# Experts of a two-layer decoder trunk: indirect DMAs for tokens and results, half of the weight loads issued by ACT, last block reordered

## The reference, cut to what matters

```python
top_logit, top_idx = lax.top_k(logits, TOP_K)          # TOP_K = 2
top_w = jax.nn.softmax(top_logit, axis=-1)
gate = jnp.einsum('tk,tke->te', top_w, jax.nn.one_hot(top_idx, N_EXPERTS, dtype=jnp.float32)).astype(u.dtype)
for e in range(N_EXPERTS):                             # 8 experts
    out = out + gate[:, e:e + 1] * swiglu(t, w_gate[e], w_up[e], w_down[e])
# swiglu: (silu(u @ w_gate) * (u @ w_up)) @ w_down, 1024 -> 3584 -> 1024
```

## Time and profile before

| | us |
|---|---|
| median of 3 runs | 1657.75 |
| lowest and highest | 1656.53, 1658.16 |
| the profiled execution's own time | 1658.17 |
| its span in the trace | 1656.4 |
| start of the item loop on PE, to the end of the last load's matmuls | 620.4 to about 1608.4 |

### The profile page before, as it was taken

The page is one execution under the profiler, slowest core; times in us unless marked ns, Lnnn a source line. Parts: engine busy times, 40 slices in busy tenths (PEclk is TensorE's granted clock), DMA queues, the critical chain, the costliest instruction groups (busy, mean ns, idle before and its releaser), DMA issues.

```text
span 1656.4 us, 21473 instructions
## 1 busy us (share of the span) xinstructions
PE 1571.4 (95%) x8127; PEld 1331.4 (80%) x8127; DVE 1293.3 (78%) x1102; ACT 1028.5 (62%) x865; POOL 17.9 (1%) x36
## 2 busy tenths in 40 slices
PE   5997999999799779999999999999999999999996
PEld 4986788887788668888888888888888888888885
DVE  4976744448686577888888888888888889889885
ACT  3545543346354636777677677677677677677663
POOL 4000000000000000000000000000000000000000
PEclk9998999999899879999999999999999999999998
DMA  7431365555344038999999999999999999999970
GB/s 232 152 128 51 110 207 200 178 178 179 126 128 140 7 115 304 376 339 358 375 339 358 375 340 358 374 341 356 375 343 356 374 342 357 374 341 358 371 277 25
DMA packets 203182, 439.70 MB, mean 265 GB/s; under 512 B 12088, under 2 KB 31104, under 8 KB 203136
## 3 DMA queue, kind: packets, MB, share of 16 engines
q1 hardware_dynamic: 200080, 437.38, 74.6%
q10 hardware_dynamic: 3056, 1.68, 0.4%
HBM read 437.98 MB, written 1.05 MB: 265 GB/s over the span
## 4 chain that ended last, share of the span: by engine, by line
PE 85%; DVE 8%; ACT 3%; SPq 2%; issue 1%; DMA 0%; DVEq 0%; ACTq 0%
PE bank L1335 26%; PE bank L1337 25%; PE bank L1336 25%; DVE wlo L803 2%; PE bank L1670 2%; PE bank L1708 1%; PE bank L1412 1%; SPq L396 1%; PE bank L1330 1%; PE bank L1486 1%; PE bank L1687 0%; ACT work L577 0%; PE bank L1688 0%; PE bank L1475 0%; ACT whi L520 0%
## 5 line engine op out<-in xcount | busy, mean ns | idle before, releaser
L803 DVE TENSOR_TENSOR wlo<-raw,whi 128x2048 fp32r<-128x2048 f32 x415 | 935.8, 2287 | 150.4 <-ACT whi L708 93.3
L708 ACT ACTIVATE whi<-raw 128x2048 fp32r<-128x2048 f32 x341 | 633.0, 1910 | 13.4 <-DMA raw<-in_w_exp_down_dram 10.0
L1335 PE MATMUL bank<-whi,uTh 128*128 128x512 f32 (+1 forms) x1312 | 517.2, 394 | 5.7 <-DVE uTl L865 4.7
L1337 PE MATMUL bank<-whi,uTl 128*128 128x512 f32 (+1 forms) x1312 | 510.1, 389 | 0.0
L1336 PE MATMUL bank<-wlo,uTh 128*128 128x512 f32 (+1 forms) x1312 | 509.4, 388 | 0.0
L1335 PEld LDWEIGHTS bank<-whi,uTh 128*128 128x128 f32 x1312 | 247.8, 189 | 55.7 <-issue 5.0
L1337 PEld LDWEIGHTS bank<-whi,uTl 128*128 128x128 f32 x1312 | 247.5, 189 | 51.6
L1336 PEld LDWEIGHTS bank<-wlo,uTh 128*128 128x128 f32 x1312 | 248.0, 189 | 48.5
L1335 PE MATMUL bank<-whi,hTr 128*128 128x512 f32 x528 | 206.1, 390 | 0.0
L1336 PE MATMUL bank<-wlo,hTr 128*128 128x512 f32 x528 | 205.5, 389 | 0.0
L1337 PE MATMUL bank<-whi,hTr 128*128 128x512 f32 x528 | 205.5, 389 | 0.0
(11 more groups left out here) (247 smaller groups left out, 1161.5 us busy)
## 6 DMA issues: line engine op xcount, KB each, us to landing
raw<-in_w_exp_gate_dram SPq DMA_DIRECT2D x112, 1024.0 KB, 5.2
raw<-in_w_exp_up_dram SPq DMA_DIRECT2D x112, 1024.0 KB, 5.2
raw<-in_w_exp_down_dram SPq DMA_DIRECT2D x112, 1024.0 KB, 4.9
raw<-in_w_in_dram SPq DMA_DIRECT2D x28, 1024.0 KB, 5.4
raw<-in_w_ffn_gate_dram SPq DMA_DIRECT2D x11, 1024.0 KB, 5.1
raw<-in_w_ffn_up_dram SPq DMA_DIRECT2D x11, 1024.0 KB, 5.2
raw<-in_w_ffn_down_dram SPq DMA_DIRECT2D x11, 1024.0 KB, 5.0
raw<-in_w_out_dram SPq DMA_DIRECT2D x8, 1024.0 KB, 5.0
```

The lines of the kernel that those rows point to most:

```text
L708: nc.scalar.activation(whi[:, s % SPLIT, :], raw[:, s % RAW, :], ACT.Copy).then_inc(hi_a, 1)
L803: return V.tensor_tensor(wlo[:, n % RAW, :], raw[:, n % RAW, :], whi[:, n % SPLIT, :].bitcast(F32), ALU.subtract).then_inc(lo_ready, 1)
L1335: T.matmul(o, sth, mvh, start=start, stop=False)
L1337: return T.matmul(o, stl, mvh, start=False, stop=stop)
```

## The change

It has three parts, all in the expert stage.

1. The normalized tokens are written once to a buffer in HBM (`tok`). For an item, the row numbers of its tokens are found by two one-column matmuls with the selection matrix (`rows_of_item`) and three small DVE operations (`rows_to_get`). POOL then issues an indirect DMA of 128 rows of 4 KB (`fetch`), and PE transposes them (`turn_tokens`, 8 transposes). An item's result leaves PSUM as fp32 (`y_out`), and POOL issues an indirect DMA that writes its 128 rows to a second buffer, `ybuf`, at places computed by `rows_to_put`. After the loop SP reads `ybuf` back in two DMAs of 1 MB, and DVE adds both rows of each token times their gate weights (`add_experts`). The gather and combine matmuls, `tokens_rest` and `add_expert` go.
2. Of the 42 loads of an item, the odd ones from 5 on (19 of them) are issued by ACT in its own program; SP issues the other 23. ACT issues load n+5 in step n, right before the `hi` of load n+4.
3. In the last block the order is g, g, u, u, d, d (of the block before), d, d. The hidden tile of `turn` has two buffers now.

```diff
@@ EXP_ORDER @@
-    EXP_ORDER += [(_k, _c, _h) for _k, _c in (("g", _r), ("d", _r - 1), ("u", _r)) for _h in range(2)]
+    EXP_ORDER += [(_k, _c, _h) for _k, _c in ((("g", _r), ("d", _r - 1), ("u", _r)) if _r < EXR - 1 else
+                                              (("g", _r), ("u", _r), ("d", _r - 1))) for _h in range(2)]
+BY_ACT = range(LEAD + 1, EXP_LOADS, 2)
@@ SP, expert(i, e) @@
-                for n, (kind, r, hf) in enumerate(EXP_ORDER):
+                for n in range(EXP_LOADS):
+                    if n in BY_ACT:
+                        continue
                     sp.wait_ge(consumed, i * EXP_LOADS + (NSTATIC + n - RAW + 1))
...
@@ SP, after the loop @@
+            sp.wait_ge(scattered, n_items * 16 + 16)
+            for t in range(TT):
+                rows2 = ybuf[t * 2 * P:(t + 1) * 2 * P, :]
+                sp.dma_start(back[t], rows2.rearrange("(p k) n -> p k n", k=2)).then_inc(yb_in[t], 16)
@@ POOL @@
+            def fetch(i, turns):
+
+                pool.wait_ge(pool_turn, turns)
+                pool.wait_ge(get_ready, i + 1)
+                nc.gpsimd.tensor_tensor(idle, spare, spare, ALU.add).then_inc(pool_turn, 1)
+                nc.gpsimd.indirect_dma_start(xg, None, tok, bass.IndirectOffsetOnAxis(ap=get_row, axis=0)).then_inc(xg_in, 16)
...
+            with pool.Fori(0, n_items) as i:
+                fetch(i + 1, i * 2 + 2)
+                pool.wait_ge(pool_turn, i * 2 + 3)
+                pool.wait_ge(put_ready, i + 1)
+                pool.wait_ge(y_ready, i * 2 + 4)
+                nc.gpsimd.tensor_tensor(idle, spare, spare, ALU.add).then_inc(pool_turn, 1)
+                nc.gpsimd.indirect_dma_start(ybuf, bass.IndirectOffsetOnAxis(ap=put_row, axis=0), ysb, None).then_inc(scattered, 16)
@@ ACT @@
+            def y_out(i):
 
                 act.wait_ge(consumed, i * EXP_LOADS + (NSTATIC + EXP_LOADS))
+                act.wait_ge(scattered, i * 16 + 16)
                 for q in range(2):
+                    nc.scalar.activation(ysb[:, q * NC:(q + 1) * NC], bank(5 + q), ACT.Copy).then_inc(y_ready, 1)
...
+            def load_next(n, i, e):
+
+                act.wait_ge(consumed, i * EXP_LOADS + (NSTATIC + n - RAW + 1))
+                to, src = expert_chunk(n, e)
+                act.dma_start(to, src).then_inc(filled[(NSTATIC + n) % RAW], 16)
+
             with act.Fori(0, n_items) as i:
+                e = act.value_load(item_expert[0:1, bass.ds(i, 1)], min_val=0, max_val=NE - 1)
                 for n, (kind, r, hf) in enumerate(EXP_ORDER):
...
                     if n == LAST_UP:
+                        act.wait_ge(consumed, i * EXP_LOADS + (NSTATIC + LAST_UP + 1))
                         tokens_hi(i + 1, 0)
                         tokens_hi(i + 1, 1)
-                        turn_hi(i, r)
+                    if n == LAST_UP + 1:
+                        turn_hi(i, EXR - 1)
+                    if n + LEAD + 1 in BY_ACT:
+                        load_next(n + LEAD + 1, i, e)
                     hi(n + LEAD, i)
-                y_hi(i)
+                y_out(i)
@@ DVE @@
+            def rows_to_get(i):
+
+                dve.wait_ge(row_ps, i + 1)
+                link_row(V.tensor_copy(row_sb, bank(7)[:, 0:1]), 5 * i + 1)
+                link_row(V.tensor_scalar(get_row, row_sb, 2.0, -2.0, ALU.max, ALU.add), 5 * i + 2)
+                V.tensor_scalar(get_row, get_row, 1, None, ALU.logical_shift_right).then_inc(get_ready, 1)
+
+            def rows_to_put(i):
+
+                link_row(V.tensor_scalar(unused, row_sb, 0.0, None, ALU.is_equal), 5 * i + 3)
+                link_row(V.tensor_tensor(unused, unused, spare, ALU.mult), 5 * i + 4)
+                dve.wait_ge(scattered, i * 16 + 16)
+                V.scalar_tensor_tensor(put_row, row_sb, -2.0, unused, ALU.add, ALU.add).then_inc(put_ready, 1)
...
+            def add_experts(t):
+
+                dve.wait_ge(yb_in[t], 16)
+                link(V.scalar_tensor_tensor(h[:, t, :], back[t][:, 0, :], g1[:, t:t + 1], h[:, t, :], ALU.mult, ALU.add))
+                V.scalar_tensor_tensor(h[:, t, :], back[t][:, 1, :], g2[:, t:t + 1], h[:, t, :], ALU.mult, ALU.add).then_inc(hacc, 1)
@@ PE @@
+            def rows_of_item(i):
+
                 pe.wait_ge(sel_ready, i * 2 + 2)
+                for t in range(TT):
+                    last = T.matmul(bank(7)[:, 0:1], sel[:, t, :], iitem[:, 2 + t:3 + t], start=t == 0, stop=t == TT - 1)
+                last.then_inc(row_ps, 1)
+
+            def turn_tokens(i):
+
+                pe.wait_ge(xg_in, i * 16 + 16)
+                for q in range(2):
+                    for c in range(4):
...
+                        last = T.transpose(bank(TOKENS[q], 4, P)[:, c, :], xg[:, k * P:(k + 1) * P], ident[:, :])
+                    last.then_inc(xT_ps, 1)
...
-                    if n in COMBINE_AT:
-                        combine(i, COMBINE_AT.index(n))
-                    if n == COMB_AT:
...
+                    if n == SELECT_AT + 1:
+                        rows_of_item(i + 1)
                     if n == LAST_UP:
...
-                        pe.wait_ge(comb_ready, i + 2)
-                        for q in range(2):
-                            gather(i + 1, q, unh, GATHER_HI, gath_hi)
-                        turn(r)
-                        for q in range(2):
-                            gather(i + 1, q, unl, GATHER_LO, gath_lo)
+                        turn_tokens(i + 1)
+                    if n == LAST_UP + 1:
+                        turn(EXR - 1)
@@ constants @@
+PUT_AT = 6
-SELECT_AT = LAST_UP - 4
+SELECT_AT = LAST_UP - 12
```

More of the change, by code:

```diff
@@ L226, in trunk @@
         exh = [region(1024 + 512 * i, NC) for i in range(2)]
-        sel = rounded("sel", 2048, TT, P)
-        combT = rounded("combT", 2304, TT, P)
-        unh = rounded("unh", 4096, TT, D)
-        unl = rounded("unl", 6144, TT, D)
+        sel = region(2048, TT, P)
+        xg = region(4096, D)
+        ysb = region(5120, D)
+        back = [region(4096 + 2048 * t, 2, D) for t in range(TT)]
         gainrow = region(8192, D)
         uTeh, uTel = uTh[:, :, 0:P], uTl[:, :, 0:P]
-        exhT = [hTr[:, i, 0:NC].rearrange("p (c n) -> p c n", c=4) for i in range(2)]
-        yeh, yel = uTh[:, :, P:2 * P], uTl[:, :, P:2 * P]
+        exhT = [[hTr[:, i, r * NC:(r + 1) * NC].rearrange("p (c n) -> p c n", c=4) for i in range(2)] for r in range(2)]
         fgain = region(9216, D)
@@ L268, in trunk @@
         iitem = stat(4)
-        gcur = stat(TT)
+        row_of, spare, row_sb, unused, idle = stat(TT), stat(1), stat(1), stat(1), stat(1)
+        get_row, put_row = (small[:, at[0] + k:at[0] + k + 1].bitcast(U32) for k in range(2))
+        at[0] += 2
         assert at[0] <= 512
@@ L725, in _ @@
                 hi(n, 0)
-            nc.scalar.activation(combT[:, :, :], ones[:, :].rearrange("p (a b) -> p a b", a=TT), ACT.Copy, scale=0.0).then_inc(comb_ready, 1)
             for t in range(TT):
@@ L1193, in _ @@
             p_lo(1)
-            for t in range(TT):
-                V.memset(gcur[:, t:t + 1], 0.0).then_inc(y_d, 1)
             choose(1)
@@ L1295, in _ @@
                     if n == LAST_UP:
-                        turn_lo(r)
                         tokens_lo(i + 1, 0)
                         tokens_lo(i + 1, 1)
+                    if n == LAST_UP + 1:
+                        turn_lo(EXR - 1)
                     lo(n + LEAD, i)
-                y_lo(i)
-            for n in range(2):
-                add_last(0, n)
+            add_experts(0)
             norm(5, 0)
-            for n in range(2):
-                add_last(1, n)
+            add_experts(1)
             gains(TURN_NORM[5], 0, norm_rows(5))
@@ L1716, in _ @@
                             pe.wait_ge(exT_ready, i * EXR + (r + 1))
+                        if r == 0 and hf == 0:
+                            pe.wait_ge(y_ready, i * 2 + 2)
                         wh, wl = chunk_in(n, 2)
@@ L1758, in _ @@
             pe.wait_ge(eul_ready, n_items * 2 + 2)
-            embed(1, tail_in(0), 0)
-            pe.wait_ge(comb_ready, n_items + 1)
-            pe.wait_ge(y_d, n_items * 2 + 2)
             for t in range(TT):
-                for n in range(2):
-                    scatter(4 + 2 * t + n, t, n)
-            embed(1, tail_in(0), 1)
+                embed(1, tail_in(0), t)
+            pe.wait_ge(y_ready, n_items * 2 + 2)
             norm(5, 0)
```

159 lines of the change are left out of this document (67 added, 92 removed).

## The result

The changed kernel takes 1815.1 us (median of 4 runs, 1799.4 to 1819.8), beside 1657.1 for the kernel before on the same chip: 1.094 times as long, with a 95% interval of 1.087 to 1.101. The forecast was 1722, range 1632 to 1775. The direction was right, the size was not: 158 us were lost where 64 had been forecast.

A forecast was written before the change was run, and what follows sets the result against it. PE was taken to bound the kernel before; with ACT's chain setting the round, an item becomes 129.9 us (+6.6). Span: 1656.4 + 53 (items) + 10 (after loop) + 1 (before) = 1720.4, with 1.4 around it 1722 us; range 1632 to 1775.

The forecast's parts named there:

- PE's 4.4 us: Expert items: dropping gather and combine matmuls cuts PE's work from 123.3 to 118.9 us per item, 35 us over eight.
- SP's latency put into a chain on ACT: ACT's item loop: each ACT issue follows the previous landing, three loads a round, so the latency SP hid is exposed.
- rival C: ACT's issuing: ACT issues only after its engine is through; item about 148 us, 1866 us in all; chance 0.05.
- So a round can't be shorter than 20.6 - 2.6 = 18.0 us.: Item rounds: three landings, `hi`, `lo` and `turn_lo` make 20.6, PE needs it 2.6 later; 16.8 us before.
- Five such rounds follow each other in an item: +6.0 us.: Item loop: 1.2 us more in each of five consecutive rounds adds 6.0 us per item.
- My own bound of 13: Item rounds: high bound, one landing in three late by a whole transfer, +2.7 per round, 13 us per item.
- The landing, 5.1: ACT's loads in the chain: issue to landing taken at the measured median of 5.1 us, three per round.
- Rival B: DMA engines: the two load streams slow each other at each meeting; item 134.6 us, 1759 in all; chance 0.20.
- The ends of the item, +1.3 and +3.7: Item start: load 5 behind `y_out`, +1.3 us; item end: gather's transfer and SP's loads delay ACT's landings, +3.7.
- The order of the last block, costed at nothing: Item's last block: PE work covers making the last hidden tile; 0, or 1 to 2 us per item if not covered.
- The ends of the kernel: After the loop: write, read back and additions, +10 us; before it: gather matmuls replaced by a DMA, +1 us.
- Rival A: Item loop: the chain has room and PE stays the bound, items of 118.9 us, 1634 in all; chance 0.20.

The follow-up runs named there:

- e1: The changed kernel with all 42 loads of an item issued by SP again; 1635.95 us, ratio 0.988 against the kernel before.
- e2: The kernel before with only ACT's issuing of the 19 odd loads from 5 on added; 1814.9 us, ratio 1.090.
- e3: The changed kernel, but ACT issues load n+6 in step n instead of n+5 (18 even loads from 6 on); 1692.3 us, ratio 1.023.
- e8: The changed kernel, but DVE makes the round's product before the `lo` that stood ahead of it; 1784.4 us, ratio 1.075.
- e6: The changed kernel with ACT's load issue moved ahead of its waits for PE's turn and the token copies; 1798.8 us, ratio 1.085.
- e12: The changed kernel with both ACT's issue ahead of its waits for PE's turn and DVE's product ahead of the `lo`; 1791.5 us, ratio 1.071.
- e9: The changed kernel, but SP's 18 even loads from 6 on bring 256 KB instead of 1 MB, ACT and DVE operations as long; 1762.3 us, ratio 1.062.
- e10: The changed kernel with two loads per round on ACT, those issued behind the wait for PE's turn back on SP; 1784.5 us, ratio 1.076.
- e11: The changed kernel with all loads issued by SP and the last block in its old order g, d, u, d; 1658.2 us, ratio 1.001.
- e5: The changed kernel, but ACT issues only loads 13, 19, 25, 31, 37, not behind PE's turn, SP the others; 1658.9 us, ratio 1.001.
- e7: The changed kernel with SP issuing everything but holding loads 9, 15, 21, 27, 33, 39 until a later slot is free; 1702.2 us, ratio 1.027.

## Why the prediction was right in direction and wrong in size

- *The bound, and PE's 4.4 us.* Right. The 118.9 us of an item were 119.0 when SP issued all loads (e1).
- *SP's latency put into a chain on ACT.* The mechanism was right: e2 shows a loss of the same size with part 2 alone, the timeline shows issue, landing, issue, and e3 takes two thirds of it back with one step of lead. ACT's sequencer does issue while the engine works, 0.2 us after the landing; *rival C* is out.
- *The step that failed: "So a round can't be shorter than 20.6 - 2.6 = 18.0 us."* As a bound it held, but I took it for the round. The path that I had written down comes to 21.2 - 2.6 = 18.6 with the landings of that round, each with 0.2 to 0.3 of passing the wait where I had 0.1. Beside it runs the path by the two `lo` and the product to the turn, also 18.6, and this one moves the turn itself. PE's waits tell which binds: 88.5 us for the product, 26.7 for the low part. In e8, with one `lo` gone from it, the other path binds, at 18.3 to 18.6; in e6 and e12 the sum of three landings fits the rounds. So opening one of these paths alone didn't free the round.
- *"Five such rounds follow each other in an item: +6.0 us."* By the means, e1's first five pieces are 84.5 us and after's 99.9: +15.4 where I had +6.0. Of these, 5 x 1.8 = 9 are the quiet round of 18.6. Of the other 6.4, the small SP loads of e9 take away 3.5, so they are landings that share the engines; 2.9 stay, in the fourth and fifth piece. The traces show where part of them comes from. POOL issues the tokens' indirect DMA of 512 KB at 713.12 us in the first item of the trace after, 1.0 us ahead of the fifth turn, and the load that ACT issues behind that turn lands after 6.5 us in the mean of seven items (6.6 in e9), against 5.1 behind the turns ahead of it. In e2, without the indirect DMAs, it is 5.1 there too, and the fifth piece is 18.9 instead of 22.6. I had this transfer at the end of the item. No run takes it out of the changed kernel, so what it costs there is not shown. My own bound of 13 was too low as well.
- *The landing, 5.1.* I took the median of one stream on one queue. ACT's mean was 6.0, and in the chain each late one counts in full. *Rival B* was nearer with 1759, and it was right as a part only: with SP's loads a quarter of the size (e9) 5.3 us of an item go, 18 stay. The Trainium skill (DMA: Bandwidth & Descriptors, Queues, rings and completion order) lets each engine take turns between queues, packet by packet. The landing of 8.5 us in e10, with 3.4 MB moved in its time, agrees with it.
- *The ends of the item, +1.3 and +3.7.* Measured 1.7 and 6.3 for the sixth and seventh piece against e1, 8.0 where I had 5.0. In the seventh the issue of load 5 stands behind `y_out`, as forecast. With small SP loads these pieces are still 14.6 and 26.1 against 12.3 and 22.2 in e1, so that most of it isn't SP's bandwidth; how it splits between the late first load and what is left over of the chain stays open.
- *The order of the last block, costed at nothing.* Wrong: it is worth 3.9 us an item in the profiled executions of e1 and e11 and 2.8 by their medians, 1.8 of the 3.9 PE's wait and 1.7 the lower clock behind it. I asked only whether the new order would be covered, and not what the old one would cost once its cover, the gather halves, was gone. The 1 to 2 us that I gave for missing cover fit the wait; the clock comes on top.
- *The ends of the kernel.* Forecast +10 and +1, measured +9.2 and -0.3. Of the first, the chain that ended last shows the parts:

```profile
1759.92 1.78 POOLq L142
1761.70 3.35 DMA ybuf<-work,small
...
1765.06 4.80 DMA work<-ybuf
```

```profile
1759.83 1.72 POOL L524 TENSOR_TENSOR small<-small 128x1 f32<-128x1 f32 x1 [45.13 <-ACT work L767]
```

The sum of the first two fits (5.1 us, 4.8 taken), its parts by luck. I had 1.5 us for POOL's add and the descriptors together and 3.3 for the write behind them. The 1.78 us are POOL's sequencer while its engine does the add of one column alone, 1.72 us. The indirect DMA starts only then, and its 3.35 us to landing include the 0.99 us of the instruction that issues it. The read took 4.8 (5.0).
- *The sum.* Eight items of +19.1 are 153, with 9 at the ends 162, against 159.2 between the spans. *Rival A* had no landing short enough (4.8 at the least, and 4.7 was its point), and by the sum above the loop by the product would still be 18.6 - 2 x 0.5 = 17.6 us with it, over PE's 16.8.
- *Two figures beside the sum.* "1675 to 1765 as this case's own range" doesn't follow from -1 to +12 us per item: with -1 the lower end is 1656.4 - 8 + 11 + 1.4 = 1661. *C*'s item of 148 isn't worked out; 19 pairs and four loads of 2.72 are 144, 1834 in all. Neither moves the forecast.

## What to carry to other kernels

An engine that consumes loads shouldn't issue the next one behind its own wait for a landing: the latency that a free-running queue hides is then paid once for each load, and one step more of lead gave back two thirds of it. When a load comes later, follow every in-order engine behind it, and ask what stands between the late item and the operation that closes a loop; here it was two `lo` ahead of the product on an engine that was 88% busy. When cover is taken away (the gather halves), price the order that remains by itself, with the clock behind a gap: without that edit, costed at nothing, nothing is left of the gain of 1.2% that e1 shows.

## What the runs showed of the hardware

- A load of 1 MB that is alone takes 5.0 us to land, of which the transfer is an estimated 2.7, by the 394 GB/s of the earlier trace rows. Between 700 and 1500 us, with two queues in use, the longest landings of such loads were 10.0 us (after) and 12.6 (e5). With SP's queue alone the median was 6.1 in e1, where it costs nothing, and 8.1 in e7, with 13.1 the longest.
- PE's granted clock was 0.81 in the 9.1 us from 982.90 in e11, which begin with a wait of 1.5 us; without that wait it was 1.00 (e1).
- POOL's add of one column ahead of the put took 1.72 us behind the last item and 0.19 in the first (763.14 us in the trace after); the put's indirect DMA of 512 KB landed 3.35 us after its start in the one and 7.9 in the other, beside a stream of weight loads.
